# HGRN2 recurrence on one core: the norm's squares through a ones matrix, and the 64- and 32-token levels in narrow array tiles

## What is computed

```python
def hgrn2_chunk(S, q, k, v, logf):
    G = jnp.cumsum(logf, axis=1)
    decay = jnp.exp(jnp.where(causal[None, :, :, None, None], G[:, :, None] - G[:, None, :], -jnp.inf))
    A = jnp.einsum('bthk,bshk,btshk->bhts', q, k, decay)
    o = jnp.einsum('bhts,bshv->bthv', A, v) + jnp.einsum('bthk,bhkv->bthv', q * jnp.exp(G), S)
...
    z = h @ w_in
    qx, fx, ix, gx = jnp.split(z, 4, axis=-1)
    f = lb + (1.0 - lb) * jax.nn.sigmoid(fx.reshape(hk).astype(jnp.float32))
    k = 1.0 - f
...
    o = rmsnorm(o, gn_g).reshape(Bsz, T, C_WIDTH).astype(h.dtype) * jax.nn.silu(gx)
    return o @ w_out, S.astype(h.dtype)
```

## Time and profile before

| | us |
|---|---|
| median of 3 runs | 3236.21 (3236.08 to 3240.31) |
| the profiled execution | 3233.23 |
| its span | 3231.5 |
| TensorE busy / weight loads | 3024.0 / 2946.3 |
| VectorE busy | 1483.2 |
| ScalarE busy | 684.1 |
| granted TensorE clock, mean | 0.967 of full |

### The profile page before, as it was taken

How to read it: one execution, slowest core, us unless ns; L and a number is a source line. 1 busy time by engine, 2 the same in 40 slices (tenths; PEclk the granted TensorE clock), 3 DMA queues, 4 the chain that set the end, 5 groups by cost and what they waited for, 6 DMA issues and landing times.

```text
span 3231.5 us, 45626 instructions
## 1 busy us (share of the span) xinstructions
PE 3024.0 (94%) x18140; PEld 2946.3 (91%) x18140; DVE 1483.2 (46%) x2545; ACT 684.1 (21%) x1112; POOL 134.9 (4%) x218
## 2 busy tenths in 40 slices
PE   6998699889999999997999999987989999999996
PEld 5997578889999999997999999986979999999996
DVE  6887674343333333337355454544253333333335
ACT  3111563121111111113112222211131111111111
POOL 4000220010000000001000000000010000000001
PEclk9999799989999999998999999987989999999998
DMA  4112322011111111111111111102111111111111
GB/s 125 46 39 65 137 73 86 33 40 40 47 40 44 42 40 52 40 36 76 46 41 41 41 41 41 41 21 86 39 40 40 41 46 40 46 40 40 53 33 59
DMA packets 47625, 162.78 MB, mean 50 GB/s; under 512 B 8432, under 2 KB 15904, under 8 KB 44624
## 3 DMA queue, kind: packets, MB, share of 16 engines
q1 hardware_dynamic: 42992, 148.45, 13.5%
q10 hardware_dynamic: 3456, 8.91, 0.8%
q0 software_dynamic: 992, 2.62, 0.4%
HBM read 142.63 MB, written 18.92 MB: 50 GB/s over the span
## 4 chain that ended last, share of the span: by engine, by line
PE 87%; DVE 6%; issue 2%; ACT 2%; POOL 1%; DMA 1%; DVEq 0%; ACTq 0%; POOLq 0%; SPq 0%
PE PS L540 20%; PE PS L542 19%; PE PS L541 19%; PE PS L782 6%; PE PS L783 6%; PE PS L784 6%; PE PS L1445 4%; DVE HF L651 1%; PE PS L1215 1%; POOL SQ L438 1%; PE PS L1186 1%; PE PS L1193 1%; PE PS L1461 1%; ACT SQ L558 1%; PE PS L1483 1%
## 5 line engine op out<-in xcount | busy, mean ns | idle before, releaser
L540 PE MATMUL PS<-HAH,WH 128*128 128x384 f32 x1872 | 649.1, 347 | 22.1 <-DVE HBL L661 6.4
L541 PE MATMUL PS<-HAL,WH 128*128 128x384 f32 x1872 | 634.1, 339 | 0.0
L542 PE MATMUL PS<-HAH,WL 128*128 128x384 f32 x1872 | 633.5, 338 | 0.0
L540 PE MATMUL PS<-HBH,WH 128*128 128x384 f32 x1872 | 626.8, 335 | 0.0
L542 PE MATMUL PS<-HBH,WL 128*128 128x384 f32 x1872 | 626.5, 335 | 0.0
L541 PE MATMUL PS<-HBL,WH 128*128 128x384 f32 x1872 | 626.5, 335 | 0.0
L528 DVE TENSOR_TENSOR WL<-WR,WH 128x1024 fp32r<-128x1024 f32 x200 | 243.0, 1223 | 565.2 <-ACT WH L523 563.6
L540 PEld LDWEIGHTS PS<-HAH,WH 128*128 128x128 f32 x1872 | 358.2, 191 | 32.1 <-issue 23.6
L782 PE MATMUL PS<-UH,WH 128*128 128x384 f32 x1056 | 360.3, 341 | 5.2 <-issue 5.0
L541 PEld LDWEIGHTS PS<-HAL,WH 128*128 128x128 f32 x1872 | 358.2, 191 | 2.7 <-issue 1.8
L783 PE MATMUL PS<-UL,WH 128*128 128x384 f32 x1056 | 359.0, 340 | 0.0
(11 more groups left out here) (206 smaller groups left out, 2620.0 us busy)
## 6 DMA issues: line engine op xcount, KB each, us to landing
WR<-w_fi_in SPq DMA_DIRECT2D x88, 512.0 KB, 3.7
WR<-w_fo_in SPq DMA_DIRECT2D x44, 512.0 KB, 3.6
WR<-w_c_in SPq DMA_DIRECT2D x32, 512.0 KB, 3.9
WR<-w_ab_in SPq DMA_DIRECT2D x20, 512.0 KB, 3.8
CACHES<-k_cache_in SPq DMA_DIRECT2D x8, 1024.0 KB, 4.8
CACHES<-v_cache_in SPq DMA_DIRECT2D x8, 1024.0 KB, 6.9
X<-x_t_in SPq DMA_DIRECT2D x3, 1536.0 KB, 10.6
x_spill<-X SPq DMA_DIRECT2D x1, 4608.0 KB, 13.0
```

Source lines behind the costliest of these rows:

```text
L540: nc.tensor.matmul(out, wh, hh(k, third(n)), start=(k == 0), stop=False)
L541: nc.tensor.matmul(out, wh, hl(k, third(n)), start=False, stop=False)
L542: mm = nc.tensor.matmul(out, wl, hh(k, third(n)), start=False, stop=(k == KT - 1))
```

## The change

The norm: `norm_sums` now has the ones matrix as the weight and the squares `AM` as the moving operand, three matmuls of 384 columns, in slot 10, so the sum of a token stands on all partitions at once. `norm_cast`, `diagonal` and their semaphores `s_cb`, `s_cd` are gone. ScalarE takes the root of the three 128x384 results into `KD` (`root(n)`), and in `finish` VectorE takes the reciprocal of each in place and multiplies it into `X`. Level 0 of the next head waits for the roots (`s_cr`) and no longer for `finish` (`s_cn`).

The levels: for lv 6 and 7 only the block pairs that count are multiplied: 16 products of 32 x 32 tokens and 8 of 64 x 64, whose outputs lie in column tiles of the array (partitions r to r+w) of one PSUM bank. VectorE takes them with four or two plain copies in place of three masked ones. `MERGES`, the number of merges of a head, falls from 24 to 20.

```diff
+WIDE = 6
+MERGES = N3 * WIDE + LEVELS + 1 - WIDE
...
@@ TensorE: vturn, level, kturn
-                if n == 0:
-                    need(pe, s_cr, T("hgrn"))
...
+                if lv >= WIDE:
+
+                    need(pe, s_mg, T("mg") - 2)
+                    T.add("mg")
+                    w = 1 << (lv - 1)
+                    for t in range(PT_TILES):
+                        for b in range(P // (2 * w)):
+                            r = w * (P // (2 * w) * (t % 2) + b)
+                            k0 = t * P + 2 * w * b
+                            mm = nc.tensor.matmul(PS[r:r + w, 3 + lv - WIDE, w * (t // 2):w * (t // 2 + 1)],
+                                                  KC[:, k0:k0 + w], QC[:, p, k0 + w:k0 + 2 * w], start=True, stop=True)
+                    mm.then_inc(s_lv, 1)
+                    return
                 for n in range(N3):
                     if lv == 0:
-                        need(pe, s_cn, T("hgrn") * N3)
+                        need(pe, s_cr, T("hgrn") * N3)
...
-                need(pe, s_mg, T("mg") - 2 + n)
+                need(pe, s_mg, T("mg") - (0 if n == 1 else 1))
@@ TensorE: the norm
             def norm_sums():
-                need(pe, s_oq, T("hgrn") * N3 + N3)
-                need(pe, s_vk, T("vk"))
-                for t in range(NT):
-                    mm = nc.tensor.matmul(PS[:, 2, TH + t:TH + t + 1], AM[:, t, :], ones[:, 0:1], start=True, stop=True)
-                mm.then_inc(s_cm, 1)
-
-            def norm_cast():
-                need(pe, s_cd, T("hgrn") + 1)
-                need(pe, s_og, T("hgrn") * N3 + N3)
+
                 for n in range(N3):
+                    need(pe, s_oq, T("hgrn") * N3 + n + 1)
+                    need(pe, s_og, T("hgrn") * N3 + n + 1)
                     mm = nc.tensor.matmul(PS[:, 3 + n, 0:TH], ones[:, :],
-                                          KD[:, TPT * n:TPT * n + TPT, :].rearrange("p a b -> p (a b)"), start=True, stop=True)
-                    mm.then_inc(s_cb, 1)
+                                          AM[:, TPT * n:TPT * n + TPT, :].rearrange("p a b -> p (a b)"), start=True, stop=True)
+                    mm.then_inc(s_cm, 1)
...
-                    if i == 11:
-                        norm_cast()
@@ ScalarE
-            def root():
-                need(act, s_cm, T("hgrn") + 1)
-                act.activation(rt[:, 0:NT], PS[:, 2, TH:TH + NT], ACT.Sqrt, bias=eps[:, 0:1], scale=1.0 / P).then_inc(s_cr, 1)
+            def root(n):
+
+                need(act, s_cm, T("hgrn") * N3 + n + 1)
+                if n == N3 - 1:
+                    need(act, s_sm, T("hgrn") + 1)
+                act.activation(KD[:, TPT * n:TPT * n + TPT, :], PS[:, 3 + n, 0:TH].rearrange("p (a b) -> p a b", b=P),
+                               ACT.Sqrt, bias=eps[:, 0:1], scale=1.0 / P).then_inc(s_cr, 1)
@@ VectorE
-                for n in range(N3):
+                if lv >= WIDE:
+                    w = 1 << (lv - 1)
+                    parts = P // w
+                    a = AM[:, 0:PT_TILES, :].rearrange("p (u two) q -> p u two q", two=2)
+                    ps = PS[:, 3 + lv - WIDE, 0:PT_TILES // 2 * w].rearrange("p (u q) -> p u q", q=w)
+                    for i in range(parts):
+                        half, b = divmod(i, parts // 2)
+                        o = 2 * w * b
+                        ins = dve.tensor_copy(a[o:o + w, :, half, o + w:o + 2 * w], ps[w * i:w * (i + 1), :, :])
+                    ins.then_inc(s_mg, 1)
+                    T.add("mg")
+                for n in range(N3 if lv < WIDE else 0):
...
-            def diagonal():
-                need(dve, s_cr, T("hgrn") + 1)
-                link(dve, T, dve.reciprocal(ri[:, 0:NT], rt[:, 0:NT]))
-                dve.tensor_tensor(KD[:, :, :], ident[:, :].unsqueeze(1).to_broadcast([P, NT, P]),
-                                  ri[:, 0:NT].unsqueeze(2).to_broadcast([P, NT, P]), ALU.mult).then_inc(s_cd, 1)
-
             def finish(h):
+
                 for n in range(N3):
-                    need(dve, s_cb, T("hgrn") * N3 + n + 1)
+                    need(dve, s_cr, T("hgrn") * N3 + n + 1)
+                    r = KD[:, TPT * n:TPT * n + TPT, :].rearrange("p a b -> p (a b)")
+                    link(dve, T, dve.reciprocal(r, r))
                     o = X[:, h, third(n)]
-                    dve.scalar_tensor_tensor(out=o, in0=o, scalar=sm("gn"), in1=PS[:, 3 + n, 0:TH], op0=ALU.mult,
-                                             op1=ALU.mult).then_inc(s_cn, 1)
+                    dve.scalar_tensor_tensor(out=o, in0=o, scalar=sm("gn"), in1=r, op0=ALU.mult, op1=ALU.mult).then_inc(s_cn, 1)
...
-                        if i == 11:
-                            diagonal()
```

More of the change, by code:

```diff
@@ L282, in encoder @@
         s_cr = sem("s_cr")
-        s_cd = sem("s_cd")
-        s_cb = sem("s_cb")
         s_cn = sem("s_cn")
@@ L1540, in c_pe @@
             with pe.Fori(0, CH // 2 - 1) as i:
-                T.enter(i, w0=2, w1=4, w2=2, up=2 * (LEVELS + 2), mg=2 * N3 * (LEVELS + 1), kt=2 * N3, vk=2 * N3, head=2, hgrn=2, sf=2)
+                T.enter(i, w0=2, w1=4, w2=2, up=2 * (LEVELS + 2), mg=2 * MERGES, kt=2 * N3, vk=2 * N3, head=2, hgrn=2, sf=2)
                 step(0, 1)
@@ L1560, in take @@
                     if n == 0:
-                        need(act, s_mg, (T("head") - 1) * N3 * (LEVELS + 1))
+                        need(act, s_mg, (T("head") - 1) * MERGES)
                     act.activation(FG[:, p, third(n)], src, ACT.Sigmoid).then_inc(s_cg[k], 1)
@@ L1622, in step @@
                     if i == 10:
-                        root()
+                        for m in range(N3):
+                            root(m)
                     if i == 11:
@@ L1659, in level @@
             def level(lv, p):
-                T.add("lv", N3)
+                T.add("lv", N3 if lv < WIDE else 1)
                 need(dve, s_lv, T("lv"))
@@ L1769, in c_dve @@
             with dve.Fori(0, CH // 2 - 1) as i:
-                T.enter(i, hi=8, gs=2 * N3, dc=2 * (1 + LEVELS + 1 + 1), lv=2 * N3 * (LEVELS + 1), mg=2 * N3 * (LEVELS + 1),
+                T.enter(i, hi=8, gs=2 * N3, dc=2 * (1 + LEVELS + 1 + N3), lv=2 * MERGES, mg=2 * MERGES,
                         ss=2 * PT_TILES, hgrn=2)
```

## The result

The changed kernel takes 3275.4 us (median of 4 runs, 3275.1 to 3276.4), the kernel before 3236.1 (4 runs, 3233.2 to 3240.3): a ratio of 1.0121, 95% interval 1.0103 to 1.0138. The profiled execution after has a span of 3273.7 us against 3231.5, 42.2 more.

What follows compares the result with a forecast made beforehand. TensorE was taken as the bound, with VectorE lacking slack at the seam of two steps. Seams +55.9 and +9.5, clock +11.4, levels -8.4, last step +1.3 made +69.7 on 3233.23: 3303 us, range 3287 to 3320.

Steps and rivals of the forecast that it cites:

- The place, the order of events and the sign: Seam of two steps: VectorE busy without gap from gate to `KC`, TensorE idle about 11 us, level 0 at half clock; slower.
- the price of a reciprocal: In `finish` on VectorE: each 384-column reciprocal takes 3.12 us, carried on from narrow ones at 7.75 ns per column.
- the seam's own arithmetic: From G, the end of a step's last product: gate at 2.20, `finish` 11.04 us, level 0 at G + 15.45.
- The lower bound of 2.78: Low end for one 384-column reciprocal in us, from the slope between 3 and 9 columns, 6.83 ns per column.
- The levels: Levels 6 and 7 in seven bodies: narrow products take 2.4 us against 3.6, -1.2 per step, -8.4 us.
- The nearest row: Attention's four column tiles, 32 loads in 0.79 us, 25 ns each, taken to price levels 6 and 7 at 0.8 us each.
- the mode switches: Entering and leaving tiled mode on TensorE at levels 6 and 7: four per head, 0.2 us each, 0.8 us.
- The clock: Low TensorE clock behind six long stalls at the seams: 1.9 us lost each, +11.4 us.
- The last step: Levels 6 and 7 without covering products save 3.0 us, the end comes 4.35 later; together +1.3 us.
- the cheap reciprocal: Rival in `finish`: a wide reciprocal costs only 0.55 us, so the kernel is not slower, 3230 us; chance 7%.

Runs made afterwards that it cites:

- widths: The changed kernel with the first third's reciprocal split into 128 and 256 columns, the second's into 48 and 336, the last whole: 3281.9 us, one run.
- no_recip: The changed kernel with a plain copy in place of each 128x384 reciprocal: 3219.2 us (3213.3 to 3222.3).

## Why the prediction was wrong

- *The place, the order of events and the sign* were right: VectorE without a gap from the gate to `KC` (but for 0.25 us at the loop's edge), TensorE idle in seven seams (8.1 to 9.4 us where a product covers, forecast 11; 13.6 in the last), released by `KC`, level 0 at half clock.
- *The failed step is the price of a reciprocal.* I carried the slope from 1 to 9 columns, 7.75 ns, over 384 and took 3.12 us; it is 2.55. In the seam's own arithmetic that explains it fully: 15.45 less 3 x 0.575 is 13.7. Over 24 reciprocals it is 13.8 us, half of the 27.6 by which the sum was too high; with the measured price alone it would have come to 3289 us, so the terms below failed too. The lower bound of 2.78 was also too high: it came from the same small widths, whose differences of 21 and 41 ns cannot carry a factor of 40. The Trainium skill (VectorE: DVE Perf Modes, First, the fixed hardware budget) has an iterative divide with a repeat count of 8; the estimate of 8.3 ns per column that I worked out from that page is not borne out: the runs have 6.25.
- *The levels were under-priced as a gain.* The nearest row, 25 ns per instruction with 128 moving columns, was too dear for 32 moving columns: 32 instructions cost 0.49 us, 15 ns each. And the mode switches, 0.8 us per head in my sum, show as 0.19. That is -15.4 in place of -8.4. The rule of the Trainium skill (TensorEngine Tiling, Instruction Overhead), some 60 cycles for any matmul, would be 25 ns at full clock, an estimate by that page; 15 ns here is below it.
- *The clock* behind the stalls was right in kind and 2.7 us too small.
- *Not in the sum:* the half clock inside bodies, 6.2 us, which the profile of before held and I had not looked for, since I read the bodies only by their length in one place. Why the changed kernel's trace has less of it stays open.
- *The last step* was +1.3 in the sum and measured -3.0. From level 6 to the transposes of `KC` it takes 4.75 us, before 8.70: 3.95 less, forecast 3.0. Levels 0 to 5, whose code did not change, are 1.8 us shorter, by the clock that they happened to have. And the end is 2.6 us later and not 4.35, by the same price of a reciprocal.
- Of the rivals, the cheap reciprocal was wrong in size, but its sign held: a copy of 0.35 us in its place gave 3219, not slower, where its arithmetic (3230 at 0.55 us, 2.4 us for every 0.1) gives 3225.

## What to carry to other kernels

An operation is worth its price only where it stands: three reciprocals per head made the seven seams 53 us longer between a gate and the next head's start, and with the same three in gaps of the same engine a few us away the seams are 5.0 us, shorter than before the change. Before moving work to an engine that is "46% busy", look for what its queue has behind it. And a duration extrapolated from small widths needs bounds as wide as the small widths' scatter times the factor.

## What the runs showed of the hardware

- VectorE's float32 reciprocal costs 6.25 ns per column with 128 partitions (446 ns for 48 columns, 2546 for 384), against 353 ns for a copy of 384 columns (runs `widths` and `no_recip`).
- Float32 products with 32-column weights and 32 moving columns, spread over four column tiles, cost about 15 ns per instruction (0.49 us for 32); with 64-column weights and 64 moving columns it was 45 ns (0.72 us for 16).
- The clock fell to 0.50 behind stretches in which TensorE was recorded as busy for 3.32 of 3.40 us, with 16-column and 32-row products; in which steps it did so differed between two profiles of one kernel. Behind as little as 2.12 us idle, level 0 ran slow as well (3.80 us in place of 2.17); behind 1.47 us it did not.
